# Conditioning in groups of four weight units, HGRN scores by a predicated copy, one activation table for ln and exp

## What is computed

```python
def ada_params(cvec, w, b):
    return jnp.split(jax.nn.silu(cvec) @ w + b, 6, axis=-1)   # w is 1024 x 6144

def hgrn2_chunk_scan(q, k, v, logf, state0):        # chunks of 32 tokens, 4 heads, 2 directions
    def step(S, xs):
        qc, kc, vc, fc = xs
        b = jnp.cumsum(fc, axis=1)
        b_mid = b[:, CHUNK // 2 - 1:CHUNK // 2]
        b_last = b[:, -1:]
        A = jnp.einsum('bthd,bshd->bhts', qc * jnp.exp(b - b_mid), kc * jnp.exp(b_mid - b))
        A = jnp.where(mask, A, 0.0)
        o = (jnp.einsum('bhts,bshe->bthe', A, vc)
             + jnp.einsum('bthd,bhde->bthe', qc * jnp.exp(b), S))
        S_new = (S * jnp.exp(b_last[:, 0])[..., None]
                 + jnp.einsum('bshd,bshe->bhde', kc * jnp.exp(b_last - b), vc))
        return S_new, o

logf_a = jnp.log(lbh + (1 - lbh) * jax.nn.sigmoid(z))
k_a = (1 - lbh) * jax.nn.sigmoid(-z)
```

## Time and profile before

| | us |
|---|---|
| median of 3 runs | 3564.25 |
| lowest, highest run | 3557.92, 3564.75 |
| span of the profiled execution | 3566.4 |
| TensorE busy (share of the span) | 2813.5 (79%) |
| VectorE busy | 929.9 (26%) |
| ScalarE busy | 406.2 (11%) |
| first layer's mixer with conditioning in it | about 110 to 682 |
| mean granted TensorE clock | 0.885 |

### The profile page before, as it was taken

The page is one execution under the profiler, slowest core; times in us unless marked ns, Lnnn a source line. Parts: engine busy times, 40 slices in busy tenths (PEclk is TensorE's granted clock), DMA queues, the critical chain, the costliest instruction groups (busy, mean ns, idle before and its releaser), DMA issues.

```text
span 3566.4 us, 31725 instructions
## 1 busy us (share of the span) xinstructions
PE 2813.5 (79%) x12336; PEld 1527.1 (43%) x12336; DVE 929.9 (26%) x2028; ACT 406.2 (11%) x759; POOL 182.3 (5%) x226
## 2 busy tenths in 40 slices
PE   5778596579979966699988777787795777877776
PEld 1434343334434433444465434433474754344333
DVE  1144715720020023420033111110354543111111
ACT  0021301110010010310001000000112111000001
POOL 1200100010000001010011000000000010000000
PEclk8898898789989988899988889988896988888888
DMA  8265854524443442044364499999640005899896
GB/s 262 89 200 172 260 161 145 169 105 146 150 147 130 141 135 80 1 159 141 118 199 185 164 371 393 379 372 378 243 142 0 5 30 214 345 376 392 368 375 284
DMA packets 319174, 724.36 MB, mean 203 GB/s; under 512 B 15074, under 2 KB 256898, under 8 KB 265198
## 3 DMA queue, kind: packets, MB, share of 16 engines
q1 hardware_dynamic: 306352, 690.01, 51.9%
q0 software_dynamic: 12736, 33.18, 2.8%
HBM read 721.94 MB, written 1.20 MB: 203 GB/s over the span
## 4 chain that ended last, share of the span: by engine, by line
PE 60%; DMA 17%; DVE 13%; ACT 4%; issue 3%; SPq 3%; POOL 1%; DVEq 0%; ACTq 0%; POOLq 0%
PE ps L770 22%; DMA ring<-in_moe_w_up 16%; PE ps L1174 8%; PE ps L795 8%; PE ps L871 7%; SPq L489 3%; PE ps L775 2%; PE ps L806 2%; PE ps L919 1%; PE ps L939 1%; PE ps L1054 1%; DVE h L1666 1%; DVE h L1664 1%; PE ps L1273 1%; DMA v_tmp<-in_norm_g 1%
## 5 line engine op out<-in xcount | busy, mean ns | idle before, releaser
L770 PE MATMUL ps<-ring,hT 128*128 128x512 f32 x1792 | 800.2, 603 | 32.0 <-DVE arena L2132 15.3
L770 PEld LDWEIGHTS ps<-ring,hT 128*128 128x128 f32 x1792 | 343.6, 194 | 455.0 <-issue 431.4
L1174 PE MATMUL ps<-arena 128*32 128x512 f32 x1536 | 297.3, 746 | 104.6 <-DMA ring<-in_moe_w_up 101.9
L1174 PE MATMUL ps<-ring,arena 128*32 128x512 f32 x512 | 296.8, 746 | 0.0
L795 PE MATMUL ps<-hT,ring 128*128 128x256 f32 (+1 forms) x1024 | 282.6, 439 | 2.3 <-ACT hT L1326 1.5
L1160 PE MATMUL ps<-arena,h 128*128 128x128 f32 x1024 | 252.4, 409 | 30.9 <-DVE arena L2157 21.6
L1160 PEld LDWEIGHTS ps<-arena,h 128*128 128x128 f32 x1024 | 246.3, 335 | 56.0 <-DVE arena L2157 46.6
L871 PE MATMUL ps<-ring,arena 128*128 128x512 f32 x592 | 260.5, 593 | 3.8 <-ACT arena L1396 3.8
L795 PEld LDWEIGHTS ps<-hT,ring 128*128 128x128 f32 x1024 | 197.5, 193 | 86.2 <-issue 61.6
L1713 DVE SCALAR_TENSOR_TENSOR arena<-ps,arena 128x256 f32<-128x256 f32 x74 | 31.9, 431 | 664.1 <-ACT arena L1392 664.0
L1174 PEld LDWEIGHTS ps<-arena 128*32 128x32 f32 x1536 | 70.2, 134 | 308.1 <-issue 199.1
(11 more groups left out here) (441 smaller groups left out, 2511.5 us busy)
## 6 DMA issues: line engine op xcount, KB each, us to landing
ring<-in_moe_w_down SPq DMA_DIRECT2D x128, 1024.0 KB, 21.3
ring<-in_ada_w SPq DMA_DIRECT2D x96, 1024.0 KB, 9.6
arena<-in_moe_w_gate SPq DMA_DIRECT2D x96, 1024.0 KB, 8.8
arena<-in_moe_w_up SPq DMA_DIRECT2D x96, 1024.0 KB, 10.9
ring<-in_ffn_w_in SPq DMA_DIRECT2D x66, 1024.0 KB, 8.5
ring<-in_ffn_w_out SPq DMA_DIRECT2D x33, 1024.0 KB, 5.1
ring<-in_moe_w_gate SPq DMA_DIRECT2D x32, 1024.0 KB, 16.4
ring<-in_moe_w_up SPq DMA_DIRECT2D x32, 1024.0 KB, 18.5
```

The source lines that it names most:

```text
L770: m = pe.matmul(o3, lhsT_of(k), ring[:, a:a + 2, k * EH:(k + 1) * EH], start=start and k == 0, stop=stop and k == KC - 1)
L1174: m = pe.matmul(ps[a * CAP:(a + 1) * CAP, 6, :].rearrange("p (u c) -> p u c", u=2), x_slots[:, k, a * CAP:(a + 1) * CAP], slot_pair(GATE_U ...
```

## The change

1. A conditioning group takes four units in place of three (`ADA_UNITS`), on column strips 0, 32, 64 and 96. There are 21 groups in place of 28. HGRN steps have 1, 1, 1, 0 groups in place of 2, 1, 2, 1; the second pair of heads has one projection group in place of two; the other places keep one group each. Which ring slots each product gets moves with that.
2. `ada_rows` adds a group's bias with one addition over partitions 0 to 96 or 97; `junk` and PSUM bank 3 are set to zero once, so that the partitions between hold numbers. GpSimd stores and loads per group, with strided rows.
3. HGRN scores are copied with `copy_predicated` under the mask into `hg_scores` (half of `h`, set to zero once). Clamp and multiplication go, and so does ScalarE's wait for `hg_out`.
4. ScalarE loads one table that has ln and exp, ahead of its wait for `hg_f`.

```diff
@@ build
+        hg_scores = h[:, 0, :].rearrange("p (d t) -> p d t", d=2)
...
-        PAIR = SLOTS * EH
-        PAIRS_PER_LAYER = 6 * D // PAIR
-        ADA_A = (2, 1) * 4
+        ADA_UNITS = 4
+        GROUPS_PER_LAYER = 6 * D // (ADA_UNITS * EH)
+        ADA_A = (1, 1, 1, 0) * 2
         ADA_B = (1,) * 8
-        PROJECTION_GROUPS = (1, 2)
+        PROJECTION_GROUPS = (1, 1)
...
-        group_rows = junk.rearrange("p (b c) -> p b c", b=2)
+        group_rows = junk[:, 0:2 * EH].rearrange("p (b c) -> p b c", b=2)
@@ SyncE, ada_groups
-                    for u, s in enumerate(n.slots(3)):
-                        fill(s, kmajor(I[name][j][:, col + 512 * u:col + 512 * u + EH]))
+                    for u, s in enumerate(n.slots(ADA_UNITS)):
+                        fill(s, kmajor(I[name][j][:, col + EH * u:col + EH * (u + 1)]))
@@ GpSimd
+            def group_bias(g):
+                name, j, _, m_, _, col = ada_group_of(g)
                 b = I[name.replace("_w", "_b")][j]
+                src = b[col:col + ADA_UNITS * EH].rearrange("(u n) -> u n", u=ADA_UNITS)
+                for r in range(m_):
+                    load(group_rows[r:r + 97:32, g % 2, :], src, sem(f"ada_bias_loaded_{g % 2}"))
...
+            def group_store(g):
+                _, _, _, m_, row, col = ada_group_of(g)
+                pool.wait_ge(sem("ada_rows_ready"), g + 1)
+                for r in range(m_):
+                    pool.dma_start(mod_dram[row + r, col:col + ADA_UNITS * EH].rearrange("(u n) -> u n", u=ADA_UNITS),
+                                   group_rows[r:r + 97:32, g % 2, :]).then_inc(sem(f"mod_stored_{g % 2}"), 16)
+                pool.wait_ge(sem(f"mod_stored_{g % 2}"), (16 if g % 2 == 0 else 0) + 16 * ada_rows_through(g))
+                if g + 2 < N_ADA:
+                    group_bias(g + 2)
@@ TensorE
-                    slots = n.slots(3)
+                    slots = n.slots(ADA_UNITS)
...
-                            m = pe.matmul(c0, T1[:, d, t * P:(t + 1) * P], v_tok[:, t, hd, 0:P],
+                            m = pe.matmul(c0, hg_scores[:, d, t * P:(t + 1) * P], v_tok[:, t, hd, 0:P],
@@ ScalarE
                 def sigmoids(i):
                     d, z = i % 2, hg_z[:, (i // 2) % 2, i % 2, :]
-                    if i >= 2:
-                        act.wait_ge(sem("hg_out"), i - 1)
                     tell(nc.scalar.activation(T1[:, d, :], z, ACT.Sigmoid), sem("act_step"))
...
                 def decays(i):
                     d = i % 2
+                    nc.scalar.preload_act_table_set("natural_log_exp_and_others")
                     act.wait_ge(sem("hg_f"), i + 1)
@@ VectorE
+            do(V.memset(junk[:, :], 0.0))
...
-                    for u in range(3):
-                        at = group_rows[32 * u:32 * u + m_, p % 2, half]
-                        ins = V.tensor_tensor(at, at, ps[32 * u:32 * u + m_, bank, half], ALU.add)
-                        do(ins) if u < 2 else tell(ins, sem("ada_rows_ready"))
+                    at = group_rows[0:96 + m_, g % 2, :]
+                    tell(V.tensor_tensor(at, at, ps[0:96 + m_, bank, half], ALU.add), sem("ada_rows_ready"))
...
+            do(V.memset(ps[:, PROJECTION_BANK, :], 0.0))
...
+            dve.wait_ge(tp_full, n.tp)
+            do(V.memset(h[:, 0, :], 0.0))
...
-                    at3 = T1[:, d, :].rearrange("p (t c) -> p t c", t=4)
-
-                    do(V.tensor_scalar(T1[:, d, :], ps[:, 4, :], MAXF, -MAXF, ALU.min, ALU.max))
-                    tell(V.tensor_tensor(at3, at3, chunk_masks[:, d:d + 1, :].broadcast_to([P, 4, P]), ALU.mult),
-                         sem("hg_scores_read"))
+                    at3 = hg_scores[:, d, :].rearrange("p (t c) -> p t c", t=4)
+
+                    tell(V.copy_predicated(at3, chunk_masks[:, d:d + 1, :].bitcast(mybir.dt.uint32).broadcast_to([P, 4, P]),
+                                           ps[:, 4, :].rearrange("p (t c) -> p t c", t=4)), sem("hg_scores_read"))
```

More of the change, by code:

```diff
@@ L356, in step_bank, with ada_group_of, ada_rows_through @@
             return {"A": 7, "B": 5}[mixer] - i % 2
-        def ada_pair_of(p):
-            l, i = divmod(FIRST_PAIRS + p, PAIRS_PER_LAYER)
+        def ada_group_of(g):
+            l, i = divmod(FIRST_GROUPS + g, GROUPS_PER_LAYER)
             name, j, rows = ADA[l]
-            return name, j, (0 if len(rows) == 2 else 2), len(rows), rows[0], PAIR * i
+            return name, j, (0 if len(rows) == 2 else 2), len(rows), rows[0], ADA_UNITS * EH * i
+        def ada_rows_through(g):
+            return sum(ada_group_of(i)[3] for i in range(g % 2, g + 1, 2))
+        ADA_STORED = [16 + 16 * ada_rows_through(2 * ((N_ADA - 1) // 2)), 16 * ada_rows_through(2 * (N_ADA // 2) - 1)]
         def row_all(ap1d):
@@ L612, in _ @@
                 load(mod_rows[q:q + 1, :], b[0:3 * D].rearrange("(o n) -> o n", o=1), sem("ada_bias_loaded_0"))
-            def pair_bias(g):
-                name, j, _, m_, _, col = ada_pair_of(g)
+            def group_bias(g):
+                name, j, _, m_, _, col = ada_group_of(g)
                 b = I[name.replace("_w", "_b")][j]
-                for u in range(3):
-                    src = b[col + 512 * u:col + 512 * (u + 1)].rearrange("(o n) -> o n", o=1)
-                    load(group_rows[32 * u:32 * u + m_, g % 2, :], src.broadcast_to([m_, 512]), sem(f"ada_bias_loaded_{g % 2}"))
-            def pair_store(g):
-                _, _, _, m_, row, col = ada_pair_of(g)
-                pool.wait_ge(sem("ada_rows_ready"), 2 * (g + 1))
-                for u in range(3):
-                    pool.dma_start(mod_dram[row:row + m_, col + 512 * u:col + 512 * (u + 1)],
-                                   group_rows[32 * u:32 * u + m_, g % 2, :]).then_inc(sem(f"mod_stored_{g % 2}"), 16)
-                pool.wait_ge(sem(f"mod_stored_{g % 2}"), (16 if g % 2 == 0 else 0) + 48 * (g // 2 + 1))
-                if g + 2 < N_PAIRS:
-                    pair_bias(g + 2)
+                src = b[col:col + ADA_UNITS * EH].rearrange("(u n) -> u n", u=ADA_UNITS)
[10 more added lines that the diff above has]
+                    group_bias(g + 2)
             pool.wait_ge(sem("mod_row_ready"), 1)
@@ L657, in _ @@
             post()
-            pairs_a = ADA_BEFORE_B // 2
-            for g in range(pairs_a):
-                pair_store(g)
+            for g in range(ADA_BEFORE_B):
+                group_store(g)
             pool.wait_ge(sem("hgrn_done"), 1)
             load(row_select, I["row_select"], sem("row_select_loaded"))
-            pair_store(pairs_a)
+            for g in range(ADA_BEFORE_B, ADA_BEFORE_B + 2):
+                group_store(g)
             pool.wait_ge(sem("ml_qk"), 4)
             load(out_g, row_all(I["ab_out_g"][0]), sem("out_g_loaded"))
-            for g in range(pairs_a + 1, N_PAIRS):
-                pair_store(g)
+            for g in range(ADA_BEFORE_B + 2, N_ADA):
+                group_store(g)
             n.h += 4
@@ L1768, in ada_rows @@
                 for g in range(g0, g0 + count):
-                    p = g // 2
-                    m_ = ada_pair_of(p)[3]
-                    dve.wait_ge(sem(f"ada_bias_loaded_{p % 2}"), (32 if p % 2 == 0 else 0) + 48 * (p // 2 + 1))
+                    m_ = ada_group_of(g)[3]
+                    dve.wait_ge(sem(f"ada_bias_loaded_{g % 2}"), (32 if g % 2 == 0 else 0) + 16 * ada_rows_through(g))
                     half = slice(EH * (g % 2), EH * (g % 2) + EH)
-                    for u in range(3):
-                        at = group_rows[32 * u:32 * u + m_, p % 2, half]
-                        ins = V.tensor_tensor(at, at, ps[32 * u:32 * u + m_, bank, half], ALU.add)
-                        do(ins) if u < 2 else tell(ins, sem("ada_rows_ready"))
+                    at = group_rows[0:96 + m_, g % 2, :]
+                    tell(V.tensor_tensor(at, at, ps[0:96 + m_, bank, half], ALU.add), sem("ada_rows_ready"))
             dve.wait_ge(x_loaded, 32)
```

15 lines of the change are left out of this document (6 added, 9 removed).

## The result

| | before | after |
|---|---|---|
| median, both kernels run on one chip, us | 3561.09 | 3595.38 |
| lowest, highest of 4 runs | 3557.73, 3564.75 | 3588.77, 3596.62 |
| ratio to before, 95% interval | | 1.0087 [1.0072, 1.0102] |
| span of the profiled execution | 3566.4 | 3594.8 |
| mean granted TensorE clock | 0.885 | 0.876 |

The change makes the kernel 34 us slower. The forecast was +11 us, 3575, with a range up to 3588: the sign was right and the time lies above the range. The two profiled executions differ by 28.4 us; the one of before stands 5 us above the median here. Those 28.4 us can be followed stage by stage; the other 6 of the 34 cannot.

The account below looks back on a forecast made before the run. Bound: a chain of waits through TensorE in the projections, a TensorE, ScalarE, VectorE loop in the HGRN, VectorE and TensorE in the mLSTM. Terms +6.4 -3.5 -10.4 +7.2 +7.4 +4 = +11.1 on 3564.25 gave 3575 us, range 3555 to 3588.

Parts of the forecast that it names:

- first projections: First token products: late slot fills, half clock behind the stop and a wait before the features; +6.4 us, +3.3 to +8.
- first HGRN step of each pair: From features' end to scores: additions, table loads and a second group leave the path; -3.5 and -10.4 us.
- other HGRN steps: Later HGRN steps: all at the half clock, about 19.4 us apart; +7.2 us for both pairs of heads.
- second projections: Second token products: the same stop, low clock and wait before features, less two additions; +7.4 us, +4.3 to +9.
- mLSTM: mLSTM groups wait for two late slot fills, cycle 12.2 us, up to 14 at low clock; +4 us, +1 to +11.
- The group of four: Conditioning groups on TensorE: four strips take 3.6 us against 3.56 for three; 4.75 was the other end.
- costless edits: The three clears and GpSimd's store, wait and bias load per group were claimed to cost nothing.
- The clock didn't stay up: Rival: TensorE's clock stays up in the HGRN, turning +7.2 into -17 us, 3551 us; chance 0.13.
- Short stops: Rival: products after stops run at full clock and the mLSTM hides its landings; 3566 us, no change; chance 0.26.
- the fourth strip is free: Its rival: the strip isn't free, groups take 4.75 us in HGRN first steps and mLSTM; +11, 3586 us; chance 0.08.
- The rival of a table switch with a hidden tail: ScalarE in the first HGRN steps: four loads leaving the path each save 1.4 us more; 3570 us; chance 0.03.
- three ring terms: Waits for ring slots in first projections, second projections and mLSTM: +6.4, +7.4 and +4 us.

Follow-up runs that it names:

- e4: The changed kernel with eight idle matmuls of 256 columns before each mLSTM group but the first; 3581.33 us, ratio 1.005.
- e7: The changed kernel with each fill of the eight mLSTM groups cut to 128 of its 256 columns, all instructions kept; 3576.77 us, ratio 1.0047.
- e5: The changed kernel with ten idle matmuls of 256 columns in each HGRN step; 3576.64 us, ratio 1.0043.
- e1: The changed kernel with groups of three units again, at their old places, keeping all HGRN edits and one addition per group; 3546.74 us, ratio 0.9953.
- e9: e1 with both token products in a row, the group behind them and the next group behind the first feature unit; 3536.7 us, ratio 0.9929.
- e8: e1 with eight idle matmuls ahead of the group in HGRN steps 1 and 5; 3538.46 us, ratio 0.9938.

## Why the prediction was right or wrong

The stages of the two profiled executions, in us. The terms are the prediction's; "after" is measured between the same events in both traces.

| term | predicted | measured |
|---|---|---|
| start of the first token product | 0 | +1.5 |
| first projections | +6.4 | +7.7 |
| features behind them | 0 | +1.5 |
| first HGRN step of each pair | -13.9 | -13.9 |
| other HGRN steps | +7.2 | +8.2 |
| second projections | +7.4 | +8.7 |
| mLSTM | +4 | +14.0 |
| end of the mixer, and all behind it | 0 | +0.7 |
| sum | +11.1 | +28.4 |

**The step that failed is the mLSTM's.** The prediction had the mechanism, the two slots of the group ahead and SyncE's waiting queue, and a cycle of "8.6 us of landing and 3.6 of group, 12.2 us, and at a low clock up to 14". It then took +4, because steps took 11 to 15 us before and 12.2 seemed to fit between them. Measured are 14.3 us on average over seven cycles, against 12.3 before, which makes 14.0. Two things were wrong in it. First, it laid the stop and the clock down as alternatives, though it had said of the projections and the HGRN that a stop of over 5 us takes the clock: here TensorE stops 5.39 us ahead of the group at 618.21, so the half clock belonged to the likeliest case and not to its edge. (Not by the length of a stop alone: the group behind a wait of 2.66 us took 5.3 us too, and the first group of the stage, behind no wait, 6.0; before, that one had 5.6.) e4 takes most of it away and gives 6.7 us back. Second, the cycle was too short even at the full clock: in e4 it is 8.6 of landing, 3.6 of group, and 0.7 of output matmuls and issue between them, which 12.2 leaves out, 13.0 us; the average step there is 13.3, against the 12.3 of before. And no step compared bytes with time. Four units are 12.0 us at 350 GB/s, three are 9.0. That alone would not have given the loss, since seven times 12.0 is 84 us, less than the 86.1 of before; it would have shown that the slack was gone, so that every pause of the fills (2.3 us of each cycle in after) lengthens the stage. e7, with half the bytes, went below before. How the last 7 us divide between the pauses and the rate of 350 GB/s can't be told by these runs, since the two bounds lie a microsecond per cycle apart.

**The projections** (+16.3 for both, 13.8 forecast) were right in kind and 2.5 us short. The slots of the first product were filled after 9.8 us and not 8.8 (fills of 6.5 and 9.1 us, where the earlier trace rows had 5.8 and 8.2). The half clock behind the stop was there, 30.65 us in place of 27.70, against 3.1 us forecast. The prediction priced the stop before the features (2.2 us forecast, 2.9 measured) without the clock behind it: the row of 188.75 to 192.00 shows 0.54, and this is the +1.5 of the features. In the second projections leaving it out turned out right: a stop of 3.5 us had the clock at 1.00 behind it.

**The first HGRN steps** came out to the tenth of a microsecond: -3.5 and -10.4. These terms were the removal of whole instructions from a chain with no other work beside it, with durations from rows.

**The other HGRN steps** came out at 18.6 and 19.4 us between states for steps 1 and 2 (19.4 was worked out for both), with output matmuls of 5.2 us behind 5.7 us of idleness (5.6 worked out). +8.2 in place of +7.2: step 1 was 0.8 shorter than its term, and step 3's states came 16.9 us behind those of step 2, not 15.9, since its state updates ran at the half clock too (2.09 us in place of 1.17), for which no row of before spoke. That this is the clock is shown by e5, where the same steps take 15.9 us.

**The group of four and the costless edits.** 3.61 us for four strips against 3.6 forecast. The copy under the predicate (0.72 us) lay inside the bounds from the neighbouring rows, and far from mattering. e7, with a stage shorter than before's, shows that stores and bias loads of GpSimd delay nothing in the mLSTM, though they are now strided.

**The rivals.** The clock didn't stay up (output matmuls of 0.77 us). Short stops did not cost only themselves (30.65 us, 5.4 us), but for the one ahead of the second features. And the fourth strip is free (3.61). The rival of a table switch with a hidden tail: in after ln starts 1.29 us after the load does (268.53 to 269.82), of which 1.28 is the load. The Trainium skill, "ScalarE: Activation LUTs", section "What ACT_TABLE_LOAD costs", adds a drain of about 1380 ns to each switch. This trace shows none, and by that rule the two first steps would have gained an estimated 5.5 us (four drains of that figure) more than the 13.9 that they did.

**The size of the range.** Most of what came out too small was a stop of TensorE and the clock behind it. The range took the parts as if they were independent, while one cause (the fourth slot) set the stops for fills: at the upper ends of the three ring terms (8, 9 and 11 for 6.4, 7.4 and 4) the sum is +21, 3585, and even that is short of 3595. The upper end of the mLSTM's own term, 11, was below the 14 measured.

## What to carry to other kernels

Before a group that shares a ring is enlarged, write down for each stage the bytes per step against the step's time at the rate that the trace shows, and how many slots stay free to be filled while the group runs. When a wait for a fill appears on a tuned matmul engine, work out the sum twice, once with the stop alone and once with the work behind it at the half clock: in after's rows the work behind stops of over 5 us began at the half clock, and behind shorter ones it sometimes did. And where edits are bundled, sum them by stage: here all edits but the fourth unit gained 14 us (e1), the fourth unit lost 49 on top of them (after less e1), and order alone (e9) was worth another 9 to 10. Compare the stage in the traces too, and not the medians alone: e4 and e8 came near their forecast times though the stage that the edit was for gained only 6.7 of 14 us and 2.6 of 8.

## What the runs showed of the hardware

- The clock can fall after the idle time is over. In e8 TensorE idled 2.29 us, ran its first two output matmuls in 0.46 us, and the next two in 0.79; in e5 it idled 1.44 us, and the clock fell some 2 us into the work (0.49 to 0.80 us for the same two matmuls). Behind the stops of 5.4 us and more in after's rows the work began at the half clock, and behind one of 3.5 us (531.10 to 534.50) at the full one.
- Idle matmuls pay where they keep the clock up: 19 us of the median in the HGRN (e5; 20.5 in the stage), 14 in the mLSTM (e4; 6.7 in the stage). In e8, with 8 in place of 10 and a stop of 2.29 us left, one of two steps gained nothing.
- Four strips of one or two stationary columns and 256 moving ones take 3.61 us where three take 3.56.
- One addition over 98 partitions and 256 columns takes 0.42 us, as long as one over 2 partitions (0.41 before).
